# A two-layer block on one Trainium2 core: weight splitting moved around four norms, and nine convolution taps in place of eleven

## What is computed

```
h = h + rms_norm(mix @ w_out, ln_attn_post)            # residual 1
hn = rms_norm(h, ln_ffn_pre)                           # norm 2
u = causal_dwconv(hn @ w_up, conv_w, conv_b)
f = (gelu(gate) * val) @ w_down
h = h + rms_norm(f, ln_ffn_post)                       # residual 3
...
h = rmsnorm(x, norm_mix_g);  proj = h @ w_in           # norm 4
a = causal_dwconv_2(a_val * sigmoid(a_gate), conv_a_w) + conv_a_b      # 31 taps
a = silu(layernorm(a, ln_a_g, ln_a_b)) @ w_a_out
x = x + merged @ w_o
x = x + memory_cross_attention(rmsnorm(x, norm_x_g), rmsnorm(mem, norm_mem_g), w_xq, w_xkv, w_xo)   # norm 6
x = x + hierarchical_moe(rmsnorm(x, norm_ffn_g), ...)
```

## Time and profile before

| | |
|---|---|
| median of 3 timed runs | 1649.49 us (1646.26 to 1649.76) |
| the profiled execution | 1644.42 us, its span 1642.6 us |
| mean granted TensorE clock | 0.981 |
| busy over the span: PE | 1517.6 us (92%) |
| PEld | 1267.1 us (77%) |
| DVE | 1099.3 us (67%) |
| ACT | 704.1 us (43%) |
| POOL | 60.6 us (4%) |

### The profile page before, as it was taken

How to read it: one execution, slowest core, us unless ns; L and a number is a source line. 1 busy time by engine, 2 the same in 40 slices (tenths; PEclk the granted TensorE clock), 3 DMA queues, 4 the chain that set the end, 5 groups by cost and what they waited for, 6 DMA issues and landing times.

```text
span 1642.6 us, 25699 instructions
## 1 busy us (share of the span) xinstructions
PE 1517.6 (92%) x10492; PEld 1267.1 (77%) x10492; DVE 1099.3 (67%) x1639; ACT 704.1 (43%) x1052; POOL 60.6 (4%) x53
## 2 busy tenths in 40 slices
PE   6999889988998999999999999999999888889992
PEld 4889676767877888888888877878788657888892
DVE  6831776777489727736779999355766435678875
ACT  5422444433454333323455222225335345367783
POOL 0000000000000000000000000000000000222221
PEclk9999999999999999999999999999999999899996
DMA  6220000002432222222323222223233202478894
GB/s 251 103 103 1 2 2 2 2 28 76 182 116 77 103 80 100 103 103 90 142 103 116 101 79 89 91 85 134 95 128 113 75 26 77 167 241 313 316 321 181
DMA packets 38803, 185.49 MB, mean 113 GB/s; under 512 B 6422, under 2 KB 6550, under 8 KB 24992
## 3 DMA queue, kind: packets, MB, share of 16 engines
q1 hardware_dynamic: 31648, 171.28, 29.7%
q0 software_dynamic: 4864, 8.40, 1.5%
q10 hardware_dynamic: 2176, 4.19, 0.7%
HBM read 178.60 MB, written 13.63 MB: 117 GB/s over the span
## 4 chain that ended last, share of the span: by engine, by line
PE 66%; DVE 21%; DMA 5%; ACT 4%; issue 3%; POOL 0%; SPq 0%; POOLq 0%; DVEq 0%; ACTq 0%
PE acc L507 18%; PE acc L509 17%; PE acc L508 17%; DMA raw<-wstream 4%; DVE wl L2063 3%; DVE CA L2549 2%; DVE wl L2051 2%; PE acc L1092 1%; ACT wh L1327 1%; ACT wh L1314 1%; PE acc L811 1%; DVE tmp L2005 1%; PE mb L656 1%; PE mb L507 1%; PE mb L602 1%
## 5 line engine op out<-in xcount | busy, mean ns | idle before, releaser
L507 PE MATMUL acc<-XH,wh 128*128 128x512 f32 x1008 | 397.7, 395 | 10.7 <-DVE wl L2063 4.3
L509 PE MATMUL acc<-XH,wl 128*128 128x512 f32 x1008 | 393.6, 390 | 0.0
L508 PE MATMUL acc<-XL,wh 128*128 128x512 f32 x1008 | 393.3, 390 | 0.0
L1327 ACT ACTIVATE wh<-raw 128x2048 fp32r<-128x2048 f32 x99 | 188.9, 1914 | 229.1 <-DMA raw<-wstream 229.1
L2063 DVE TENSOR_TENSOR wl<-raw,wh 128x2048 fp32r<-128x2048 f32 x99 | 225.7, 2286 | 57.5 <-ACT wh L1327 54.6
L507 PEld LDWEIGHTS acc<-XH,wh 128*128 128x128 f32 x1008 | 189.8, 188 | 54.8 <-issue 7.4
L508 PEld LDWEIGHTS acc<-XL,wh 128*128 128x128 f32 x1008 | 189.8, 188 | 40.6 <-issue 1.9
L509 PEld LDWEIGHTS acc<-XH,wl 128*128 128x128 f32 x1008 | 189.6, 188 | 39.6
L1348 ACT ACTIVATE ev<-acc 128x512 f32<-128x512 f32 x146 | 84.9, 596 | 225.6 <-PE acc L509 171.9
L2051 DVE TENSOR_TENSOR wl<-raw,wh 128x1024 fp32r<-128x1024 f32 x96 | 116.6, 1223 | 31.0 <-ACT wh L1314 30.6
L1314 ACT ACTIVATE wh<-raw 128x1024 fp32r<-128x1024 f32 x96 | 101.0, 1060 | 20.6 <-DMA raw<-wstream 19.1
(11 more groups left out here) (535 smaller groups left out, 2745.5 us busy)
## 6 DMA issues: line engine op xcount, KB each, us to landing
raw<-wstream SPq DMA_DIRECT2D x99, 1024.0 KB, 4.9
raw<-wstream SPq DMA_DIRECT2D x96, 512.0 KB, 6.0
YG<-YT ACTq DMA_DIRECT2D x8, 512.0 KB, 6.2
XT<-xT SPq DMA_DIRECT2D x2, 1024.0 KB, 9.6
XT<-xT SPq DMA_DIRECT2D x1, 2048.0 KB, 7.7
GMT<-memT SPq DMA_DIRECT2D x2, 1024.0 KB, 8.3
XD<-HN SPq DMA_DIRECT2D x4, 512.0 KB, 3.4
out<-XTK SPq DMA_DIRECT2D x4, 512.0 KB, 2.6
```

The costliest lines, as they stand in the source:

```text
L507: mm(out_, a[0], b[0], start=start, stop=False)
L508: mm(out_, a[0], b[1], start=False, stop=False)
L509: return mm(out_, a[1], b[0], start=False, stop=stop)
L1327: actv(wh[:, n % RING].rearrange("p a b c -> p (a b c)"), raw[:, n % RING, :], ACT.Copy).then_inc(hi_done, 1)
```

## The change

Five places are edited. (1) `TAPS` goes from 11 to 9: eight of the 124 taps move from the start of `mix` to the last `some_taps`. (2) At residuals 1 and 3 ScalarE makes the upper parts of the next stage's second and third block right after `values_out`, at m = 1 and m = 5, within the loop; only the fourth block's stays behind it. (3) The lower part of block 19 is made ahead of the last two squares of `out`, not behind the reciprocal. (4) The lower part of block 55 is made at m = 6 of the last feed-forward group, not behind the reciprocal. (5) In `kx`, the four pairs of the queries' operand follow each other on VectorE and ScalarE, and the parts of blocks 92 (lower) and 93 (both) come after them.

```diff
-TAPS = 11
+TAPS = 9
...
                 if m in (1, 5):
                     values_out(0, m // 4)
-            for n in (B0["v0"], B0["v0"] + 1, B0["ffn"]):
-                ahead(n)
+                    ahead(B0["v0"] + m // 4)
+            ahead(B0["ffn"])
             norm_root(2)
...
                 if m in (1, 5):
                     values_out(1, m // 4)
-            for n in (B0["v1"], B0["v1"] + 1, B0["mix"]):
-                ahead(n)
+                    ahead(B0["v1"] + m // 4)
+            ahead(B0["mix"])
             norm_root(4)
...
             for b in range(4):
-                if b == 3:
-                    operand_upper(6, 0)
-                    operand_upper(6, 1)
-                ahead(B0["kx"] + b)
-                if b == 3:
-                    operand_upper(6, 2)
-                    operand_upper(6, 3)
+                if b < 3:
+                    ahead(B0["kx"] + b)
+                else:
+                    for k in range(4):
+                        operand_upper(6, k)
...
             for k in range(4, KT):
                 operand_upper(6, k)
+            ahead(B0["kx"] + 3)
...
                 if m == 5:
                     memory_lowers(0)
+                    lows(B0["out"] + 6)
             norm_recip(1)
-            lows(B0["out"] + 6)
...
                     if last and name == "ffn" and m >= 2:
                         add_squares(24 + m - 2)
+                    if last and name == "ffn" and m == 6:
+                        low(B0["mix"])
...
             norm_recip(3)
-            low(B0["mix"])
...
             norm_recip(6)
-            lows(B0["kx"] + 2 + 3)
             dve.wait_ge(rb_ready, 7)
-            operand_pair(6, "norm_x", 0)
+            for k in (0, 2, 4, 6):
+                operand_pair(6, "norm_x", k)
             lows(B0["kx"] + 3 + 3)
-            for k in (2, 4, 6):
-                operand_pair(6, "norm_x", k)
             lows(B0["q"] + 3 + 3)
```

## The result

| | before | after |
|---|---|---|
| median, same comparison | 1649.22 us (1646.26 to 1650.41) | 1636.63 us (1631.33 to 1641.05) |
| ratio | | 0.9926 (0.9909 to 0.9943) |
| the profiled execution | 1644.42 us, span 1642.6 | 1639.76 us, span 1637.9 |
| mean granted TensorE clock | 0.981 | 0.978 |

The kernel is 12.6 us faster by the medians, 12.2 by the ratio. Two later comparisons of the same two kernels gave ratios of 0.9948 (0.9929 to 0.9966) and 0.9932 (0.9908 to 0.9956), that is 8.6 and 11.2 us. The mean of the 85 later runs of the kernel before is 1647.9 us (standard error 0.3) and that of all 22 runs of the changed kernel 1637.4 us (0.9): the change is worth about 10.5 us (1.0). Chip by chip, the means of the two later comparisons differ by 9.6 and 11.6 us. I had said 7.7.

The account below looks back on a forecast made before the run. TensorE bounds the kernel between 425 and 1300 us, so only its gaps count. 0 (B) + 1.5 + 1.7 + 0.3 (C) - 2.0 (D) + 4.8 - 0.8 (A) + 2.2 (E) = 7.7 us: 1641.8 us, range 1637.5 to 1646.6.

Parts of the forecast that it names:

- The clock term: Behind the accumulator gap, shrunk from 4.18 to about 3.0 us, the clock would not fall: 1.7 us gained.
- I take the difference as it stands: Profiled execution 5.1 us below the timed median; same difference assumed for both kernels, so 7.7 us is subtracted from 1649.49.
- B: First norm, lower part ahead of the last squares: fits VectorE's 3.84 us wait, costs nothing and gains nothing.
- C: Upper parts within residuals: first norm 1.5 us plus 1.7 us of clock; second norm 0.3 us.
- a sign of being wrong: Wrong if VectorE's first lower part behind the residual still starts later than 1.3 us after the sixth step.
- the first rival: Clock still falls behind the 3.0 us gap, or falls elsewhere: 6.0 us gained, 1643.5 us; chance 0.18.
- the fourth rival: A split within the residual meets a load not landed: 12.1 us slower, 1661.6 us; chance 0.02.
- D: Second norm, lower part ahead of the last squares: VectorE has no pause, TensorE stands still, 2.0 us lost.
- the second rival: D costs nothing because a square, not the lower part, is last: 9.7 us gained, 1639.8 us; chance 0.10.
- A: Nine taps for eleven: mix gaps of 0.72 and 3.60 us go, 4.8 us gained; 0.8 lost at the layer norm's sum.
- the third rival: Mix gaps turn into another wait, on accumulator takes behind ScalarE: 3.6 us gained, 1645.9 us; chance 0.17.
- E: Queries' operands together in kx: the 1.94 us gap at 1252.21 goes, 2.2 us gained.

Follow-up runs that it names:

- last two kernels: Changed kernel without the fourth edit: ScalarE empties accumulator tiles 2 and 3 before the first GELU, 1633.8 us; then also block 23's lower part one block earlier, 1633.01 us.
- filled kernel: Kernel before, with small matmuls into an unused bank during its two long gaps (feed-forward, mix), waits unchanged: 1646.53 us, ratio 0.9982.

## Why the prediction was right in direction and short in size

**The clock term is the step that failed.** "The gap of 3.60 us at 956.03 is followed by no such stretch, so I take it that 3.0 us doesn't cost the clock", and with it "I take the difference as it stands". The conclusion for 3.0 us held, but by luck, since the premise didn't: the gap of 3.60 us does cost the clock, in most executions. So the sum had the clock behind the gaps of 3.60 and 1.94 us at nothing, because one execution showed none. All 14 traces together, by the gap in front:

| gap, place | traces with a fall behind it | lost when it falls |
|---|---|---|
| 4.1 to 4.2 us, accumulator | 5 of 5 | 1.7 us |
| 3.4 to 3.6 us, `mix` | 4 of 5 | 1.5, 1.7, 2.6 and 3.0 us |
| 3.0 us, accumulator | 0 of 6 | |
| 1.8 to 2.2 us, queries | 3 of 6 | 1.7 us |
| 1.8 and 2.2 us, feed-forward, last two kernels | 0 of 2 | |
| 1.7 us, second norm's sum | 1 of 4 | 1.7 us |
| long ones filled | 0 of 1 each | |

(Six traces have the queries' gap; one of them is of the filled kernel, which left it alone.) In these 14 segments no fall stands anywhere else: each begins between 1.6 us before the end of a gap of this table and 2.4 us behind it, and the gaps of up to 1.3 us never had one. The 2.4 us are those of the one fall at the second norm, so that its tie to that gap is the weakest. The mean loss behind the gap of `mix` is (0 + 1.5 + 1.7 + 2.6 + 3.0) / 5 = 1.8 us (what I expected of the changed kernel's third comparison has 3.4 us twice, which counts the part of a fall in which TensorE still stood idle), behind the queries' gap 0.5 x 1.7 = 0.9, behind the new one at the second norm 0.25 x 1.7 = 0.4. So the nine taps are worth 1.8 us more than in my sum, the queries' operands 0.9 more, and the fourth edit costs 0.4 more: 7.7 + 1.8 + 0.9 - 0.4 = 10.0 us beside the measured 10.5. The terms I had put at 4.8 and 2.2 us for the gaps should have been about 6.6 and 3.1. The counts are small, so these means carry some half a microsecond each. Their total is borne out by the timed runs: 1.7 + 1.8 + 0.9 - 0.4 = 4.0 us of clock, measured 4.5 (1.2).

It also explains part of the 5.1 us by which the profiled execution lay below the median, which I noted and did not use: the clock kept at two gaps that often lose it is worth 2.7 us on average, and by its own clock the execution lost 31.8 us, 1.7 less than the mean. I should have read that difference as a sign that the execution lacked some loss, and asked which. What remains of the first comparison, 12.6 against 10.5, is within its spread; the later two lie on both sides of 10. With 10.5 us the time would have been 1639.0, inside the range: the last 2 us of the miss are chance, and of the 2.8 us before them 2.3 are the clock by these counts.

The Trainium skill (TensorE: Matmul & The Clock Gate, Part 1) says that the monitor behind the clock runs free of the kernel, so that the slow start of one and the same kernel differs from run to run. The traces show the like at gaps within the kernel: granted clock 1.00 and 0.64 behind the same 3.60 us. I had applied that sentence only to the fall that I saw, not to the ones that I didn't.

**B, free: right.** In the changed kernel the lower part runs at 445.18 inside the wait for the squares, and 1.64 us of wait are still left behind it, against 3.84 in the earlier trace rows. VectorE's timeline:

```profile
445.18 2.28 DVE L2062 TENSOR_TENSOR wl<-raw,wh 128x2048 fp32r<-128x2048 f32 x1
...
449.10 1.49 DVE L1979 TENSOR_TENSOR sqa<-sqa,sq 128x512 f32<-128x512 f32 x2 [1.64 <-ACT sq L1604]
```

**C, first norm: right.** ScalarE's second moved part, and VectorE behind it:

```profile
472.49 1.91 ACT L1327 ACTIVATE wh<-raw 128x2048 fp32r<-128x2048 f32 x1
474.30 0.72 ACT L1386 ACTIVATE XRH<-XT,par 128x512 fp32r<-128x512 f32 x1
476.56 1.91 ACT L1327 ACTIVATE wh<-raw 128x2048 fp32r<-128x2048 f32 x1
```

```profile
475.05 0.75 DVE L2037 SCALAR_TENSOR_TENSOR XRL<-XT,par,XRH 128x512 fp32r<-128x512 f32 x1 [2.46 <-ACT XRH L1386]
476.18 0.75 DVE L2037 SCALAR_TENSOR_TENSOR XRL<-XT,par,XRH 128x512 fp32r<-128x512 f32 x1 [0.38 <-ACT XRH L1386]
476.84 6.69 DVE L2062 TENSOR_TENSOR wl<-raw,wh 128x2048 fp32r<-128x2048 f32 x3
```

TensorE's sums of k = 5 and k = 6, with the first matmul of k = 6 between them:

```profile
474.86 1.02 PE L602 MATMUL mb<-sq,cst 128*128 128x512 f32 x2
475.85 0.50 PE L507 MATMUL acc<-XRH,wh 128*128 128x512 f32 x1
...
477.35 1.02 PE L602 MATMUL mb<-sq,cst 128*128 128x512 f32 x2
```

The part delays the residual's upper part by its own 1.8 us. The step from one sum to the next is 2.49 us here where the others are 2.25, so TensorE loses 0.2 us at k = 6, inside the 0 to 0.3 forecast and too little to be drawn as a gap. The first lower part starts 1.0 us behind the start of k = 6, under the 1.3 us that I had named as a sign of being wrong, and the three lower parts follow the last low at once: the 2.69 us of the earlier trace rows are gone, and 1.5 us of them reach the accumulator gap as forecast, 4.18 becoming 2.98 with the 0.36 us gap gone as well. At the second norm the small gap is gone too, and the same step takes 2.50 us. No fall followed in 6 of 6 traces, so the 1.7 us came with it and the first rival is out. No load was late: the fourth rival is out too.

**D, the loss: right.** 1.68 us and the 0.16 under the matmul before it, 1.8 against my 2.0, with the square sums as releaser; the second rival is out. That a fall can follow such a gap, as at 841.6, I had not foreseen.

**A: right in its gaps.** Both lower parts' gaps are gone and no other wait took their place, so the third rival falls; the layer norm's sum waits 0.58 + 0.16 us, against 0.8. **E: right.** The gap is gone and nothing new stands near it.

With the clock falls taken off, the segment shows the gaps alone. In the two traces of before 870.6 - 1.7 and 873.5 - 5.1 are 868.9 and 868.4 us; in the three of the changed kernel 862.0, 862.4 and 862.4. That is 6.4 us beside the 6.0 that I summed without the clock, and the 6.0 of the timed runs: the steps had the gaps right within 0.4 us. This also disposes of the rival that some edit saves work I had not seen.

## What to carry to other kernels

Where TensorE is the bound, price a gap as its length plus the mean clock loss behind it, and take that mean from several traces of the same kernel: one trace shows a fall or none, and either alone misleads. When the profiled execution lies well below the median of the timed runs, ask which loss it was spared before you subtract a difference from that median. Work moved onto an engine that has no pause at that place shows up as a stall for its whole length, even when the timed difference is too small to see; here 2.28 us of moved work cost 1.8 us, and leaving it in place was better.

## What the runs showed of the hardware

Idle gaps that I would have passed as harmless were followed by TensorE at 1.2 instead of 2.4 GHz in part of the executions: 3 of 6 at 1.8 to 2.2 us, and 1 of 4 at 1.7 us. One of 3.0 us never was in six traces. So length alone does not order them, and what else does is open. With a gap filled by 128-column matmuls the clock stayed at 2.4 GHz behind it, in the one trace of each of two gaps, and the timed runs lost 3.3 us less to the clock. And the spread between runs of one kernel, 1643.3 to 1659.1 us over 85 runs, goes about half with the clock: the correlation of 0.73 with the lost time stands for 0.54 of the variance.
